# Value columns of the retention mixer by seven block products out of eight, placed first, with weight tiles, modulation slabs and fills placed anew

## The reference, cut to what matters

```python
RET_HEADS = 4; RET_DK = 256; RET_DV = 512            # q, k: 1024 columns each; v, g: 2048 each

def odd_mixer(h_ctx, h_lat, w_in, w_out, cos, sin, need_ctx):     # need_ctx is False here
    p = split_parts(h_lat @ w_in, ODD_PARTS)                      # q, k, v, g of the 256 tokens
    pc = project_parts(h_ctx, w_in, ODD_PARTS, ['k', 'v'])        # k and v of the context too
    ...
    s_fw = retention_final_state(k_c, v_c, log_g_fw)
    s_bw = retention_final_state(flip(k_c), flip(v_c), log_g_bw)
    ...
    o_fw, _ = retention_chunked(q_l, k_l, v_l, log_g_fw, s_fw)
    o_bw, _ = retention_chunked(flip(q_l), flip(k_l), flip(v_l), log_g_bw, s_bw)
    return None, gated_head_norm(o_fw + flip(o_bw), p['g']) @ w_out
```

## Time and profile before

| what | us |
|---|---|
| median of three runs | 2795.39 |
| the profiled execution, its own time | 2794.11 |
| its span in the trace | 2791.8 |
| PE busy | 2687.6 (96%) |
| DVE busy | 1540.6 (55%) |
| ACT busy | 666.4 (24%) |
| odd projections, 861.61 to 1118.24 of the trace | 256.6 |

### The profile page before, as it was taken

The page is one execution under the profiler, slowest core; times in us unless marked ns, Lnnn a source line. Parts: engine busy times, 40 slices in busy tenths (PEclk is TensorE's granted clock), DMA queues, the critical chain, the costliest instruction groups (busy, mean ns, idle before and its releaser), DMA issues.

```text
span 2791.8 us, 36195 instructions
## 1 busy us (share of the span) xinstructions
PE 2687.6 (96%) x14412; PEld 2020.8 (72%) x14412; DVE 1540.6 (55%) x3100; ACT 666.4 (24%) x1727; POOL 0.2 (0%) x4
## 2 busy tenths in 40 slices
PE   6989899999999999999999999999999999999999
PEld 2545656888886444689978657769997855776999
DVE  4856657655864520146646644426773664443775
ACT  3144512111002000212111341223312143222330
POOL 0000000000000000000000000000000000000000
PEclk9999999999999999999999999999999999999999
DMA  8531015455576653256643311125663422114563
GB/s 339 179 85 51 34 31 166 151 179 168 201 260 249 254 211 120 66 144 168 183 154 121 121 61 61 61 91 154 171 192 123 151 75 77 60 43 139 152 177 126
DMA packets 335124, 387.35 MB, mean 139 GB/s; under 512 B 10972, under 2 KB 264044, under 8 KB 322412
## 3 DMA queue, kind: packets, MB, share of 16 engines
q1 hardware_dynamic: 332220, 378.14, 41.4%
q10 hardware_dynamic: 2736, 6.89, 0.7%
HBM read 383.96 MB, written 1.05 MB: 138 GB/s over the span
## 4 chain that ended last, share of the span: by engine, by line
PE 79%; DVE 9%; issue 5%; DMA 4%; ACT 3%; SPq 0%; ACTq 0%; DVEq 0%
PE acc L759 23%; PE acc L810 11%; PE acc L798 10%; PE mx L759 10%; PE acc L824 7%; PE acc L1078 2%; PE acc L840 2%; PE acc L1061 2%; DVE arena L2186 2%; DVE arena L2913 1%; PE mx L931 1%; DMA mod_w<-in_mod_w 1%; PE mx L1351 1%; PE mx L945 1%; DMA mod_w<-in_w_ada 1%
## 5 line engine op out<-in xcount | busy, mean ns | idle before, releaser
L798 PE MATMUL acc<-ring,hT 128*128 128x512 f32 x832 | 361.7, 595 | 5.9 <-ACT hT L1658 4.6
L759 PE MATMUL acc<-arena 128*128 128x128 f32 (+1 forms) x2056 | 322.6, 299 | 2.1 <-ACT gate L1890 0.8
L810 PE MATMUL acc<-hT,ring 128*128 128x256 f32 (+1 forms) x1280 | 307.0, 401 | 2.8 <-ACT hT L1568 1.3
L798 PEld LDWEIGHTS acc<-ring,hT 128*128 128x128 f32 x832 | 157.6, 191 | 205.4 <-issue 199.5
L759 PEld LDWEIGHTS acc<-arena 128*128 128x128 f32 x2056 | 282.7, 192 | 16.1 <-DVE arena L2541 1.5
L2186 DVE SCALAR_TENSOR_TENSOR arena<-mod_w,vcols,arena 128x2048 f32<-128x2048 f32 x98 | 228.4, 2348 | 111.9 <-DMA mod_w<-in_w_ada 100.7
L810 PEld LDWEIGHTS acc<-hT,ring 128*128 128x128 f32 x1280 | 242.1, 190 | 66.1 <-issue 30.8
L824 PE MATMUL acc<-ring,hT 128*128 128x512 f32 x512 | 245.5, 606 | 0.9 <-ACT hT L1568 0.9
L2538 DVE TENSOR_TENSOR arena<-ring 128x512 f32<-128x512 f32 (+1 forms) x136 | 91.7, 675 | 201.6 <-PE acc L759 185.9
L759 PE MATMUL acc<-hT,ring 128*128 128x128 f32 (+1 forms) x1208 | 187.1, 304 | 8.9 <-DVE hT L2553 3.8
L759 PE MATMUL acc<-arena,ring 128*128 128x128 f32 (+1 forms) x1160 | 182.9, 300 | 4.1 <-DVE x L2679 2.2
(11 more groups left out here) (366 smaller groups left out, 3511.1 us busy)
## 6 DMA issues: line engine op xcount, KB each, us to landing
ring<-in_w_in SPq DMA_DIRECT2D x28, 2048.0 KB
mod_w<-in_w_ada SPq DMA_DIRECT2D x48, 1024.0 KB, 5.6
ring<-in_ffn_w_in SPq DMA_DIRECT2D x88, 512.0 KB
ring<-in_w_up SPq DMA_DIRECT2D x88, 512.0 KB
mod_w<-in_mod_w SPq DMA_DIRECT2D x40, 1024.0 KB, 5.0
ring<-in_odd_w_in SPq DMA_DIRECT2D x12, 2048.0 KB
ring<-in_ffn_w_out SPq DMA_DIRECT2D x16, 1024.0 KB
ring<-in_w_down SPq DMA_DIRECT2D x16, 1024.0 KB
```

Of the source, the lines that this page charges most:

```text
L759: ins = nc.tensor.matmul(out, w[:, k, :], h[:, k, :], start=start and k == 0, stop=stop and k == n - 1, skip_group_check=more)
L798: ins = nc.tensor.matmul(b[:, 0:width], src[:, k, P * i:P * (i + 1)], w[:, k, :], start=k == 0, stop=k == KD - 1)
L810: ins = nc.tensor.matmul(b[:, 0:hi - lo], w[:, k, P * f:P * (f + 1)], hT[:, k, lo:hi], start=k == 0, stop=k == KD - 1)
```

## The change

1. **Values (`retention_values`, new).** The v columns are computed first in the odd mixer, before q, k and g. Four weight tiles give eight units. A unit is a pair of 256 tokens (unit `q` takes the token half `q % 2` and the tile `q // 2`), and is computed by seven products of four 256-column matmuls, at L792 of the kernel after. A unit has three copies and one result on ACT, and three results on DVE (L2890, L2894, L2898). Before a tile is used, DVE makes four sums of 128 x 1024 of it (L2858 to L2864); the sums of the inputs are made once (L2872 to L2877). SP may issue the tile two further on when both units of a tile are through (`rv_z`, incremented by product 3).
2. **Slabs of the odd mixer.** DVE takes two slabs in each unit and the rest ahead of the heads' rotary embedding; SP's list and the places of PE's sums follow.
3. **Even mixer.** Of the ten slabs that SP issued ahead of the first head's weights, four go out behind these. In the last slots of its loop DVE and PE finish a unit one slot earlier (`units_out`).
4. **Start of every feed-forward network.** DVE makes the first input sum as soon as the first half of the normed input is there. The first network has no slab in its first step, and a slab in each step but one after it.
5. **Second block.** In attention, fills go into 29 of slots 0 to 31 (not 6, 12, 18) where they went into slots 0 to 28, and the cumulated gates come two slots later. In the decay part fills of 4, 3, 3 become 3, 3, 2, and four of the inversion's levels get a fill of one step each.

```diff
-MOD_SUM_AFTER = {"even": (13,), "odd": (8, 15, 24, 38)}
+MOD_SUM_AFTER = {"even": (13,), "odd": (2, 6, 18, 30)}
-MOD_UP_SUM, MOD_DOWN_SUM = {8: 3, 18: 4}, {3: 5, 7: 6, 11: 7}
-MOD_ODD = (12, 5, 5, 6)
+MOD_UP_SUM, MOD_DOWN_SUM = {9: 3, 19: 4}, {3: 5, 7: 6, 11: 7}
+MOD_UNITS, MOD_ODD = (2, 2, 2, 2, 2, 2, 2, 2), (6, 2, 2, 2)
 def up_slabs(q):
-    return 1 if q != 8 and q < 21 else 0
+    return 1 if q not in (0, 9) and q < KF else 0
+def units_out(slot):
+    lag = 4 if slot < UNITS else 3
+    return [o for o in ([slot - 4, slot - 3] if slot == UNITS else [slot - lag]) if 0 <= o < UNITS]
-    a.slab_tile = [first] * 4 + [first + 2] * 10 + [first + 8] * 2
+    a.slab_tile = [first] * 4 + [first + 2] * 6 + [first + 4] * 4 + [first + 8] * 2
+    for c in range(4):
+        a.ring_used("unit", 2 * c + 2, 2)
...
+                def product5(q):
+                    pe.wait_ge(rv_t, 4 * (q // 2) + 2)
...
+                def product3(q):
+                    pe.wait_ge(rv_t, 4 * (q // 2) + 4)
+                    pe.wait_ge(rv_c11, q + 1)
+                    product(z_(q), A[q % 2][1][1], rv_weight_sums(q // 2)[2], False, True, more=True).then_inc(rv_z, 1)
...
+                for q in range(1, units):
+                    if q > 1:
+                        product1(q)
+                    product5(q)
+                    product4(q - 1)
+                    product6(q)
+                    product2(q)
+                    product3(q - 1)
+                    mod_after("odd")
+                    product7(q)
...
+            retention_values(2)
             for lo in (256, 256, 0, 0):
                 by_feature(4, lo, 512, where="odd")
-            for tok in (BOTH,) * 4 + (LAT,) * 4:
-                by_token(tok, 512, where="odd")
+            for _ in range(4):
+                by_token(LAT, 512, where="odd")
...
-                    if u < 29:
+                    if u < 32 and u not in (6, 12, 18):
                         fill(1, hT, LAT)
...
-                        fill(4, hT, LAT)
+                        fill(3, hT, LAT)
...
-                            fill(3, hT, LAT)
+                            fill(3 - j, hT, LAT)
...
+                        if level < 5:
+                            fill(1, hT, LAT)
...
                     if q == 0:
+                        dve.wait_ge(h_ready, KD * use + KD // 2)
+                        inputs_summed(in0, B, h_sums(w), (0,))
                         dve.wait_ge(h_ready, KD * (use + 1))
-                        inputs_summed(in0, [[h[:, :, e, 512 - width + w * t:512 - width + w * (t + 1)] for t in range(2)]
-                                            for e in range(2)], h_sums(w))
+                        inputs_summed(in0, B, h_sums(w), (1, 2, 3))
...
+            def value_weights_summed(c, only=(0, 1)):
+                t3, t2, t4 = rv_weight_sums(c)
+                t = pl.tile["ret_v"] + 2 * c
+                b = rv_tile(t)
+                if 0 in only:
+                    need(dve, rv_z, 2 * c - 2)
+                    dve.wait_ge(w_in[t // 2 % RING], pl.landed[t][1])
+                    V.tensor_tensor(t3, b[0][0], b[0][1], ALU.subtract).then_inc(rv_t, 1)
+                    V.tensor_tensor(b[0][1], b[0][1], b[1][1], ALU.add).then_inc(rv_t, 1)
+                if 1 in only:
+                    dve.wait_ge(rv_t, 4 * c + 2)
+                    V.tensor_tensor(t2, b[0][1], b[0][0], ALU.subtract).then_inc(rv_t, 1)
+                    dve.wait_ge(rv_t, 4 * c + 3)
+                    V.tensor_tensor(t4, b[1][0], t2, ALU.subtract).then_inc(rv_t, 1)
...
+            for q in range(10):
+                if 1 <= q < 9:
+                    o = q - 1
+                    dve.wait_ge(rv_u3s, o + 1)
+                    V.tensor_tensor(rv_out(o, 1, 1), seven(2 + o % 3, 256), u3[:, o % 2], ALU.add).then_inc(rv_c11, 1)
+                if q >= 2:
+                    o = q - 2
+                    dve.wait_ge(rv_z, o + 1)
+                    V.tensor_tensor(rv_out(o, 1, 0), seven(2 + o % 3, 256), u2[:, o % 2], ALU.add).then_inc(rv_c10, 1)
+                if q < 8:
+                    dve.wait_ge(rv_p2, q + 1)
+                    dve.wait_ge(rv_p1s, q + 1)
+                    V.tensor_tensor(rv_out(q, 0, 0), seven(5, 256), p1[:, q % 2], ALU.add).then_inc(rv_c00, 1)
+                    if q % 2 == 0 and q < 6:
+                        value_weights_summed(q // 2 + 1)
+                    mod_slabs(MOD_UNITS[q])
```

More of the change, by code:

```diff
@@ L242, in block_order @@
 def block_order(use):
-    return (0, 2, 4, 6, 1, 3, 5, 7) if use % 2 else range(KD)
+    return (0, 2, 4, 6, 1, 3, 5, 7) if use % 2 or use == 2 else range(KD)
 def mod_conds(g):
@@ L303, in make_plan @@
     a.free_jobs("norm2", 1)
[L304 to L306 removed]
+    a.start("ret_v")
+    for c in range(4):
+        a.ring_used("unit", 2 * c + 2, 2)
+    tiles("odd", (("ret_q", [4, 4]), ("ret_k", [4, 4]), ("ret_g", [2] * 4)))
+    a.slab_tile += [a.tile["ret_v"] + n for n in (0, 0, 2, 2, 2, 2, 4, 4, 4, 4, 6, 6, 6, 6, 8, 8, 8, 8, 10, 10, 10, 10,
+                                                  12, 12, 14, 14, 16, 16)]
     a.free_jobs("ret_oT", KD)
@@ L604, in _ @@
                           KD * 2 + 1: pl.tile["ffn0"] + 3}
-            released = {"job": acc_full, "part": w_part, "pair": st_z, "down": st_d}
+            released = {"job": acc_full, "part": w_part, "pair": st_z, "down": st_d, "unit": rv_z}
             def load_slabs(t):
@@ L686, in _ @@
             down_chunks(a["ffn_w_out"][0])
-            for c in range(12):
+            for c in (4, 5, 6, 7, 0, 1, 2, 3, 8, 9, 10, 11):
                 load(wcols(a["odd_w_in"][0], 512 * c, 512 * c + 512))
@@ L1319, in seven_products, with retention_values, x_, z_ @@
                 pe.wait_ge(st_e, emp0 + 28)
+            def retention_values(use):
+                stage("ret_v")
+                emptied(job.n)
+                fresh[0] = None
+                h = by_parity(hT)
+                A = [[[h[:, :, e, 256 * pair + P * i:256 * pair + P * (i + 1)] for e in range(2)] for i in range(2)]
+                     for pair in range(2)]
+                B = {}
+                units = 8
+                def x_(q):
+                    return seven(q % 2, 256)
+                def z_(q):
+                    return seven(2 + q % 3, 256)
+                def product1(q):
+                    if q % 2 == 0:
+                        first = tile.n
+                        weights(512)
+                        B[q // 2] = rv_tile(first)
+                    if q >= 2:
+                        pe.wait_ge(rv_c01, q - 1)
+                    product(x_(q), A[q % 2][0][0], B[q // 2][0][0], True, True,
+                            (lambda k: pe.wait_ge(h_ready, KD * use + k + 1)) if q == 0 else lambda k: None).then_inc(rv_p1, 1)
+                def product2(q):
+                    need(pe, rv_c00, q)
+                    product(seven(5, 256), A[q % 2][0][1], B[q // 2][1][0], True, True,
+                            (lambda k: pe.wait_ge(h_ready, KD * use + KD // 2 + k + 1)) if q == 0
+                            else lambda k: None).then_inc(rv_p2, 1)
+                def product5(q):
+                    pe.wait_ge(rv_t, 4 * (q // 2) + 2)
+                    if q < 2:
+                        pe.wait_ge(rv_s, 4 * q + 1)
+                    if q >= 3:
+                        pe.wait_ge(rv_c10, q - 2)
+                    product(z_(q), rv_sums(q % 2)[0], B[q // 2][0][1], True, True)
+                def product6(q):
+                    pe.wait_ge(rv_t, 4 * (q // 2) + 3)
+                    if q < 2:
+                        pe.wait_ge(rv_s, 4 * q + 3)
+                    pe.wait_ge(rv_p1s, q + 1)
+                    product(x_(q), rv_sums(q % 2)[2], rv_weight_sums(q // 2)[1], False, True, more=True).then_inc(rv_p6, 1)
+                def product7(q):
+                    pe.wait_ge(rv_u2s, q + 1)
+                    product(x_(q), rv_sums(q % 2)[1], rv_weight_sums(q // 2)[0], False, True, more=True).then_inc(rv_p7, 1)
+                def product4(q):
+                    if q < 2:
+                        pe.wait_ge(rv_s, 4 * q + 4)
+                    pe.wait_ge(rv_u3s, q + 1)
+                    product(x_(q), rv_sums(q % 2)[3], B[q // 2][1][1], False, True, more=True).then_inc(rv_x, 1)
+                def product3(q):
+                    pe.wait_ge(rv_t, 4 * (q // 2) + 4)
+                    pe.wait_ge(rv_c11, q + 1)
+                    product(z_(q), A[q % 2][1][1], rv_weight_sums(q // 2)[2], False, True, more=True).then_inc(rv_z, 1)
+                product1(0)
+                product1(1)
+                product2(0)
+                product5(0)
+                product6(0)
+                product7(0)
+                for q in range(1, units):
[8 more added lines that the diff above has]
+                    product7(q)
+                product4(units - 1)
+                product3(units - 1)
+                mod_after("odd")
+                pe.wait_ge(rv_c00, units)
```

(5 more changed lines are left out.)

75 lines of the change are left out of this document (63 added, 12 removed).

## The result

The kernel before took 2793.11 us in the median of six runs (2790.43 to 2796.78), the changed kernel 2802.74 in the median of six (2800.02 to 2807.61). The ratio is 1.0034, with a 95% interval of 1.0024 to 1.0044: slower by 9.6 us, or 0.34%. Forecast were 13.9 us slower, 2809, with a range from 2782 to 2817.

A forecast was written before the change was run, and what follows sets the result against it. PE was taken to bound the kernel, busy 96% of the span. Terms +19.7 +0.7 -2.4 -2.0 -2.5 +0.4 gave +13.9 us on a median of 2795.4, so 2809, range 2782 to 2817.

The forecast's parts named there:

- The values' work: Odd mixer's values on PE: 16 jobs (110.0 us) replaced by 56 products (96.7), a change of -13.3 us.
- terms for start and end: Value stretch: 3.5 us of waits at the start against 2.7 before, and 1.9 at the end, +2.7 together.
- The waits: Value stretch: PE waits at product 3 for DVE's `c11`, 3.2, 6.9, 7.5 and 5.9 us, together +23.5.
- The estimate of 6.8: Landing time of a 2 MB value tile by the skill's DMA rule, 6.8 us; the forecast used 8.2 instead.
- The clock: Value stretch: PE's clock falls after each of four waits, costing about 1.7 us each, +6.8.
- The start of the networks: Feed-forward networks: first network's waits of 1.52 and 1.31 us shrink, -2.4; three later networks give -2.0.
- The second block: Second block's mixers: attention -1.25 us for each of two layers, decay and inversion +0.4, -2.1 forecast.
- Decay and inversion: Second block: decay loses fill steps worth 3.4 us, inversion gains 3.4, plus small waits, +0.4 (bounds -1 and +3).
- The even mixer: Even mixer: the wait for first head's weights goes, but slots wait for DVE instead, +0.7 us (bounds -1 and +4).
- the odd mixer's part: Odd mixer's new values: work, waits, start, end and clock together, +19.7 us.
- a sign: Value stretch: DVE's first sum of a value tile (L2858) should wait some 6 to 8 us twice, named DMA.
- the three waits of PE: Value stretch: PE at L792 should wait three times for 6 to 8 us behind DVE L2890.

The follow-up runs named there:

- Both-edits kernel: Changed kernel with a value tile's sums made one unit later on DVE and slabs taken out of units 2, 4, 6 and 7: 2772.87 us, ratio 0.9926.
- The experiments with sums and slabs: Changed kernel with only the tile's sums moved a unit later, 2794.34 us; with only the slabs out of units 2, 4, 6 and 7, 2784.3 us.
- The idle matmuls: Changed kernel with six unused fp32 matmuls of 512 columns on PE ahead of product 3 of units 2, 4 and 6: 2795.26 us.
- the other parts alone: Kernel before with the edits to even mixer, feed-forward networks and second block, odd mixer as it was: 2784.41 us, ratio 0.9968.
- the old attention put back: Kernel with later tile sums and moved slabs, second block's attention as before (fills in slots 0 to 28, gates two slots earlier): 2775.91 us.
- the old fills: Kernel with later sums and moved slabs, decay and inversion as before: 2771.11 us; with even-mixer idle matmuls too, 2771.18 against 2773.77 with the new ones.
- the kernel without slabs: Changed kernel with slabs taken out of units 2, 4, 6 and 7, tile sums left in place: 2784.3 us, ratio 0.9969.
- with the wait filled: Kernel with later tile sums and moved slabs, plus four and three idle matmuls in the even mixer's two waits: 2773.77 us.

## Why the prediction held, and where it was off

- **The values' work, -13.3.** Both-edits kernel: 10.7 less in the odd mixer, and the step's own terms for start and end (+2.7) make up the rest to 0.1. With the waits (22.8) and the clock (8.8) of the next two points, -10.7 comes to +20.9, and the odd mixer's stage shows +21.2.
- **The waits, +23.5.** Measured 22.8, one by one 2.68, 6.94, 7.44, 5.73 against 3.2, 6.9, 7.5, 5.9. The landing was 8.2 as read from the earlier trace rows, and the end of `c11` came 17.1 after the issue (17.3). The experiments with sums and slabs show that both stand in the wait: without either it shrinks, and without both it is gone. The estimate of 6.8 for such a tile, worked out from the fit in the Trainium skill, "DMA: Bandwidth & Descriptors" (Anatomy of one DMA), would have put the waits 1.4 too low; the page measured that fit on GpSimd's path, and this tile goes by SyncE's queue. The measurement goes with the rows.
- **The clock, +6.8.** By the granted clock in the slices the four falls lost 1.7, 2.6, 1.7 and 2.8, together 8.8. The term was right in kind and 2.0 too small. Behind unit 0 the clock fell once PE was back and stayed low for 3.4, as in the earlier trace rows. In units 2, 4 and 6 it fell 1.6, 3.5 and 1.1 before PE was back and stayed low for 6.8 each time, so that 5.2, 3.3 and 5.7 of it fell on PE's work; I had not priced a longer fall. The idle matmuls show that it is a cost of its own: 7.5 came back in the medians, with product 3 of unit 2 starting 16.8 after the tile's issue, for 17.2 without them. The loss behind those three waits is 7.1 by the slices, where I had put 7.5 on record.
- **The start of the networks.** The first wait went from 1.52 to 0.42, and that of 1.31 went wholly: 2.4, as forecast. The stage lost 4.0 in the trace and 3.3 with the other parts alone. The rest are waits of 0.2 to 0.7 in the down products (L2679, L2541) that come in some traces and not in others; I had no term for them.
- **The second block, -2.1 forecast.** "I take -1.25 for each of two layers" for the attention: undone, it costs 3.0 in the medians and 2.3 to 5.0 against the traces with the new attention. The 7.2 of the first pair is close to the widest difference that two of the traces show. So this step was too small by up to 2.5; I had counted the waits of the earlier trace rows alone. The traces show what was left out. PE idles little less in the last slots (3.3 in the first layer before, 2.7 with both edits, waits over 0.25 counted), but the clock is another. Slices around these slots, first before, then with both edits (the third column from the end is the granted clock):

```profile
1630.00:1644.00 14.00, 11.49 (x43) 8.86 (x42) 4.43 (x18) 7.64 (x19) 0.00 (x0) 0.51 0.18 69
```

```profile
1616.00:1630.00 14.00, 11.44 (x58) 7.35 (x57) 5.02 (x21) 9.53 (x23) 0.00 (x0) 1.00 0.43 152
```

In each layer the clock is at 1.2 GHz for 13.7 us before and for 10.2 with the old attention put back, and for 0 to 6.8 in every trace with the new one. So the fills in the last slots save clock as well as waits. How much of the time is the clock's no run tells apart.
- **Decay and inversion, +0.4.** The stage shows 0.0; the medians show 1.8 and 2.6 in favour of the old fills, with intervals that overlap. Whether there is a difference, and what makes it, stays open.
- **The even mixer, +0.7.** Within the spread of the runs, so its size is not shown. In the changed kernel the wait for the weights went, and waits of 0.5 and 1.3 at the sum of slabs came in its place.

In the medians the odd mixer's part cost 18.3 for 19.7 forecast, and the other parts gave 8.9 for 5.8: these two differences, 1.4 and 3.1, make 4.5, against the 4.3 by which the total was over. The mechanism held, with waits that come out to 0.7 of the sum. That the total came so near owes something to chance: in the changed kernel's trace the odd mixer is 1.5 over the forecast and the rest of the kernel some 8 under it. What I had as a sign, DVE's first sum waiting 6 to 8 us, was 9.5 and 9.4: DVE was already idle before the tile was issued. Of the three waits of PE that I had at 6 to 8, the last was 5.73.

## What to carry to other kernels

When a transfer is released by an engine's progress, look at what stands first in another engine's order on that transfer, and at what stands behind it: a sum that is needed two units later, placed a unit early, made PE wait for a tile that it did not need yet. Moving it a unit later and the slabs out of the way turned 9.6 us of loss into 20 of gain, 8.9 of them from the other parts. Price a wait of PE of some 3 us and more with the slow clock behind it, look at the clock also where short waits stand close together, and before filling it to hold the clock, ask whether PE or another engine ends the stretch that follows.

## What the runs showed of the hardware

- A wait of 2.5 to 2.8 on PE does not always cost clock: in the kernel without slabs, the product behind 2.69 took 3.59 and the one behind 2.52 took 3.04, but the one behind 2.81 took 1.97, with the clock at full throughout.
- In the even mixer of the kernel before, the clock fell 0.3 after PE was back from a wait of 4.5 and stayed at 1.2 GHz for 17.1 us. PE was busy for most of them, almost all with matmuls of 64 and 128 columns; two waits of 1.51 and 0.49 stood among them. Behind the waits in the value stretch, where 256-column products followed at once, 2.4 GHz came back 3.3 to 5.7 us after PE did. The narrow matmuls do not lower the clock by themselves: with the wait filled, the same pairs of 64 columns ran at 2.4 GHz (0.39 for 0.63 us). Whether they keep a clock low that has fallen was not tried.
- No single long wait is needed: in the second block's attention before, waits of 0.45 to 1.03 among narrow matmuls went with a clock at 1.2 GHz for 13.7 us in each layer.
